# A hybrid decoder step: the recurrent heads' preparation moved beside the output gate's columns, which become two groups of four banks

## What is computed

```python
x = x + 0.5 * swiglu1(rmsnorm(x))
proj = rmsnorm(x) @ w_in          # split: q_a, k_a, v_a, f_a | qk_m, v_m, o_m, i_m, f_m
y_a = per-head rmsnorm(attention with forget gates over q_a, k_a, v_a)
qk_c = silu(causal_conv(qk_m))    # width 4, 2048 channels: 8 heads of q, 8 of k
h_m, C, n, m = mlstm(q_m, k_m, v_m, gates, state_C, state_n, state_m)
y_m = sigmoid(o_m) * per-head rmsnorm(h_m)
x = x + concat(y_a, y_m) @ w_out
x = x + 0.5 * swiglu2(rmsnorm(x))
```

## Time and profile before

| what | value |
|---|---|
| median of 3 runs | 2315.3 us (2314.76 to 2317.62) |
| the profiled execution, its time | 2320.72 us |
| its span | 2319.1 us |
| busy TensorE / VectorE / ScalarE / GpSimd | 2290.2 / 1228.4 / 842.8 / 50.3 us |
| TensorE's granted clock, mean | 0.994 |
| transfers, mean | 166 GB/s, 384.05 MB |

### The profile page before, as it was taken

How to read it: one execution, slowest core, us unless ns; L and a number is a source line. 1 busy time by engine, 2 the same in 40 slices (tenths; PEclk the granted TensorE clock), 3 DMA queues, 4 the chain that set the end, 5 groups by cost and what they waited for, 6 DMA issues and landing times.

```text
span 2319.1 us, 48002 instructions
## 1 busy us (share of the span) xinstructions
PE 2290.2 (99%) x17805; PEld 2246.8 (97%) x17805; DVE 1228.4 (53%) x1907; ACT 842.8 (36%) x1109; POOL 50.3 (2%) x84
## 2 busy tenths in 40 slices
PE   9999999999999999999999999999999999999998
PEld 8999999999999999887999989999999999999997
DVE  6554444355444455467456766755554434554443
ACT  4333333333333343334334433533333333333332
POOL 2000000000000010010000110000000000000000
PEclk9999999999999999999999999999999999999999
DMA  6555555555554444547445455455554445555443
GB/s 169 180 166 164 164 164 175 166 166 163 171 166 166 165 152 146 168 136 271 157 164 167 132 155 173 151 181 163 163 163 168 171 168 169 168 164 168 164 163 131
DMA packets 176901, 384.05 MB, mean 166 GB/s; under 512 B 19133, under 2 KB 44853, under 8 KB 176501
## 3 DMA queue, kind: packets, MB, share of 16 engines
q1 hardware_dynamic: 173888, 375.99, 50.4%
q0 software_dynamic: 2512, 5.57, 0.8%
q10 hardware_dynamic: 416, 1.32, 0.2%
HBM read 373.09 MB, written 9.70 MB: 165 GB/s over the span
## 4 chain that ended last, share of the span: by engine, by line
PE 95%; DVE 3%; ACT 1%; DMA 0%; issue 0%; SPq 0%; POOL 0%; ACTq 0%; DVEq 0%; POOLq 0%
PE ps L1788 30%; PE ps L1786 30%; PE ps L1787 29%; DVE w_lo L1010 1%; PE ps L2044 1%; DMA w_raw<-in_w_up 0%; ACT w_hi L632 0%; PE ps L2057 0%; PE ps L1856 0%; PE ps L1857 0%; PE ps L1863 0%; PE ps L1990 0%; PE ps L2337 0%; PE ps L1979 0%; PE ps L2245 0%
## 5 line engine op out<-in xcount | busy, mean ns | idle before, releaser
L1010 DVE TENSOR_TENSOR w_lo<-w_raw,w_hi 128x1024 fp32r<-128x1024 f32 (+2 forms) x698 | 789.7, 1172 | 983.9 <-ACT w_hi L632 982.5
L632 ACT CAST w_hi<-w_raw 128x1024 fp32r<-128x1024 f32 (+2 forms) x698 | 670.6, 1008 | 1290.3 <-PE ps L1788 1284.7
L1786 PE MATMUL ps<-x_hi,w_hi 128*128 128x288 f32 (+1 forms) x2752 | 813.0, 295 | 4.4 <-DVE w_lo L1010 2.6
L1788 PE MATMUL ps<-x_hi,w_lo 128*128 128x288 f32 (+1 forms) x2752 | 813.9, 296 | 0.0
L1787 PE MATMUL ps<-x_lo,w_hi 128*128 128x288 f32 (+1 forms) x2752 | 807.7, 293 | 0.0
L1786 PEld LDWEIGHTS ps<-x_hi,w_hi 128*128 128x128 f32 x2752 | 517.5, 188 | 6.3 <-DVE w_lo L1010 3.0
L1787 PEld LDWEIGHTS ps<-x_lo,w_hi 128*128 128x128 f32 x2752 | 521.2, 189 | 0.1
L1788 PEld LDWEIGHTS ps<-x_hi,w_lo 128*128 128x128 f32 x2752 | 516.5, 188 | 0.0
L1786 PE MATMUL ps<-hid_hi,w_hi 128*128 (+1 forms) x1376 | 405.6, 295 | 1.4 <-DVE X L1243 1.4
L1788 PE MATMUL ps<-hid_hi,w_lo 128*128 (+1 forms) x1376 | 407.0, 296 | 0.0
L1787 PE MATMUL ps<-hid_lo,w_hi 128*128 (+1 forms) x1376 | 403.8, 293 | 0.0
(11 more groups left out here) (487 smaller groups left out, 1438.1 us busy)
## 6 DMA issues: line engine op xcount, KB each, us to landing
w_raw<-in_w_down SPq DMA_DIRECT2D x178, 512.0 KB
w_raw<-in_w_gate SPq DMA_DIRECT2D x320, 256.0 KB
w_raw<-in_w_up SPq DMA_DIRECT2D x320, 256.0 KB
w_raw<-in_w_in SPq DMA_DIRECT2D x64, 512.0 KB
w_raw<-in_w_in SPq DMA_DIRECT2D x64, 384.0 KB
page<-in_cache_k SPq DMA_DIRECT2D x16, 512.0 KB, 4.6
w_raw<-in_w_out SPq DMA_DIRECT2D x16, 512.0 KB
w_raw<-in_w_gate SPq DMA_DIRECT2D x32, 192.0 KB
```

The lines of the kernel that those rows point to most:

```text
L632: nc.scalar.copy(w_hi[:, slot, 0:width], w_raw[:, slot, 0:width]).then_inc(w_hi_ready, 1)
L1010: nc.vector.tensor_tensor(w_lo[:, slot, 0:width], w_raw[:, slot, 0:width], w_hi[:, slot, 0:width].bitcast(F32), ALU.subtract).then_inc(w_l ...
L1786: mm(out, hi, x_hi[:, k, :], start=first and pair == 0 and s == slots[0], stop=False)
L1788: ins = mm(out, lo, x_hi[:, k, :], start=False, stop=last and pair == 1 and s == slots[-1])
```

## The change

in_m keeps three groups (q, k, v). The gate's 1024 columns become in_o, two groups of 512 columns in banks 0 to 3. The preparation is cut into pieces that stand behind banks of these groups' products and use banks 4 to 7. A step is a pair of slots, 16 in all. The convolutions, which had stood beside the groups of v and o, are now beside those of k and v: conv_tiles says which. The sigmoid of om is in two halves: the first beside step 9, the second in the third head (h = 2). qw is now made by GpSimd. Buffers on the right side of SBUF are in another order, since they lie over xm, which is still in use; state 0 is loaded as soon as w_used says that the place is free. Ws moves into counts, kws and vws into xt.

```diff
-    mixer = [("in_a", 4, KD, KD, plain[:6]), ("in_m", 4, KD, KD, plain),
+    mixer = [("in_a", 4, KD, KD, plain[:6]), ("in_m", 3, KD, KD, plain),
+             ("in_o", 2, KD, KD, plain[:4]),
...
+    def conv_tiles(t):
+        first = (0, 0, 2, 5)[t] if t < 4 else 2 * t
+        return range(first, (0, 2, 5, 8)[t] if t < 4 else first + 2)
...
         def load_out():
             load_turn(a.turn, range(SLOTS), columns(wo, 0, a.width))
+            sp.wait_ge(w_used, O_MOST)
+            load_state(0)
...
 # GpSimd
+        pool.wait_ge(w_used, O_MOST)
+        for x in qw:
+            nc.gpsimd.memset(x[:, :, :], 0.0).then_inc(sem("km_ready"), 1)
...
 # ScalarE
+            split_pair(g.turn + g.turns + (t + 1), 0, width)
+            for j in conv_tiles(t):
+                conv_silu(j)
+            split_pair(g.turn + g.turns + (t + 1), 2, width)
...
+        for step in range(16):
+            if step >= 1:
+                split_o(step + 1)
...
+            if step == 9:
+                sigmoid(0)
+            if step == 10:
+                act.wait_ge(sem("ws_logits"), 1)
+                nc.scalar.activation(Ws, Ws, ACT.Exp).then_inc(sem("ws_exp"), 1)
+            if step == 15:
+                act.wait_ge(w_used, O_MOST)
+                for i in range(2):
+                    act.wait_ge(sem("kmsT_done"), i + 1)
+                    nc.scalar.copy(kms[:, i * 512:(i + 1) * 512], ps[:, 7 - 2 * i, :]).then_inc(sem("kms_ready"), 1)
+        split_o(17)
...
             num_out(h)
+            if h == 2:
+                sigmoid(1)
 # VectorE
-        for i in range(4):
-            if i < 2:
-                split_turns(g, g.turn + i * g.turns, g.turns, UW)
+        for i in range(3):
+            width = UW if i < 2 else IN_O.width
+            if i == 0:
+                split_turns(g, g.turn, g.turns, UW)
             else:
                 for t in range(g.turns):
-                    conv((i - 2) * H + 2 * t)
-                    conv((i - 2) * H + 2 * t + 1)
+                    for j in conv_tiles((i - 1) * g.turns + t):
+                        conv(j)
...
+            if step == 7:
+                in_o_out(0)
...
+            if step == 12:
+                dve.wait_ge(w_used, O_HALF)
+                v_apart(0)
+                k_weighted(0)
+            if step == 13:
+                k_weighted(1)
+                v_apart(1)
+            if step == 14:
+                k_weighted(2)
+                k_weighted(3)
+        in_o_out(1)
+        split_o(17)
 # TensorE
+        def beside_o1(step, b):
+            if step == 0 and b == 2:
+                s_spread()
+            if step == 1 and b < 2:
+                v_natural(b, 4 + b)
+            if step == 2 and b < 2:
+                pe.wait_ge(sem("s_all_ready"), b + 1)
+                v_natural(2 + b, 6 + b)
...
+        def beside_o2(step, b):
+            if step == 2 and b == 0:
+                pe.wait_ge(sem("vws_ready"), 1)
+                pe.wait_ge(sem("ya_scaled"), 1)
+                by_sequence(vws, 0, 4, "vsT_done")
...
+        for i, beside in ((0, beside_o1), (1, beside_o2)):
+            for kt in range(IN_O.turns):
+                turn_products(IN_O, IN_O.turn + i * IN_O.turns, IN_O.index + i, kt, xm_hi, xm_lo, kt == 0,
+                              kt == IN_O.turns - 1, xr, beside)
...
         def scores(h):
...
-                pe.wait_ge(sem("kw_ready"), 2)
+                pe.wait_ge(banks_free, G_O * NBANK + 2)
```

More of the change, by code:

```diff
@@ L285, in build @@
     G_A, G_M, G_O = groups["in_a"].index, groups["in_m"].index, groups["out_a"].index
+    IN_O = groups["in_o"]
+    O_HALF, O_MOST = ((IN_O.turn + IN_O.turns + n) * 2 + 2 for n in (2, 3))
     OUT_A, OUT_B, OUT_M = groups["out_a"], groups["out_b"], groups["out_m"]
@@ L922, in _ @@
[L922 to L929 removed]
+            width = UW if t < 2 * g.turns - 1 else IN_O.width
@@ L2152, in _ @@
             turn_products(g, g.turn, g.index, kt, xm_hi, xm_lo, kt == 0, kt == g.turns - 1, xr, ya_sample_sums)
[L2153 removed]
+        with pe.Fori(1, 3) as i:
             group_products(g, i, xm_hi, xm_lo, xr)
[L2157 to L2162 removed]
@@ new lines, in v_natural, with rows_natural @@
+        def v_natural(i, bank):
+            (t, n), half = TT[i // 2], i % 2
+            for j in range(4):
+                ins = tr(ps[0:n, bank, j * P:(j + 1) * P], vm[:, 4 * half + j, t * P:t * P + n], ident[:, :])
+            ins.then_inc(sem("vT_done"), 1)
+        def rows_natural():
+            for a, row in enumerate((r_row, ws_row)):
+                for t, n in TT:
+                    ins = tr(ps[0:n, 6, (3 * a + t) * H:(3 * a + t + 1) * H], row[:, t * P:t * P + n], ident[0:H, 0:H])
+            ins.then_inc(sem("nat_done"), 1)
@@ new lines, in conv_natural, with k_natural, by_sequence @@
+        def conv_natural(i, bank):
+            for j in range(4):
+                ins = tr(ps[0:27, bank, j * P:(j + 1) * P], conv_last[:, 4 * i + j, :], ident[:, :])
+            ins.then_inc(sem("conv_rows_done"), 1)
+        def k_natural(i, bank):
+            for j in range(4):
+                ins = tr(ps[:, bank, j * P:(j + 1) * P], ext[:, H + 4 * (i % 2) + j, i // 2 * P:(i // 2 + 1) * P], ident[:, :])
+            ins.then_inc(sem("kT_done"), 1)
+        def by_sequence(src, i, bank, made):
```

313 lines of the change are left out of this document (176 added, 137 removed).

## The result

The changed kernel takes 2323.70 us by the median of 11 runs (2320.21 to 2327.35), the kernel before, timed on the same chip, 2317.56 us (11 runs, 2314.76 to 2317.98). The ratio is 1.0029 with a 95% interval of 1.0021 to 1.0037: slower by some 6 us, outside the forecast's range of 2310.8 to 2318.6. The change was timed a second time in a later session, with 2323.16 against 2316.56 and a ratio of 1.0025 (1.0016 to 1.0034). The forecast had started from 2315.3, the median of three runs; by eleven runs the same kernel's median is 2.3 us higher.

A forecast was written before the change was run, and what follows sets the result against it. TensorE, busy 2290.2 of 2319.1 us, was taken to bound the kernel. The terms -3.3 - 0.9 + 0.5 + 2.4 = -1.3 gave 2317.8, or 2314.0 as the runs' median; range 2310.8 to 2318.6.

The forecast's parts named there:

- The half clock gone, -3.3: Between input projection and head 0: vm transposes, L2168 and L2161 move between products at full clock, saving 3.3 us.
- the carry: From profile to runs: the median's 0.23% lead over the profiled execution (2315.3 against 2320.7) carries over, 2317.8 becoming 2314.0.
- Idles gone, -0.9, new idle +0.5: TensorE before head 0: two idles of 0.88 us in all go; scores(0) newly waits 0.5 us for evicted banks.
- The third convolutions, +2.4: Second in_m group, turns 2 and 3: third convolution waits for a Silu, stalling TensorE 0.9 and 1.5 us.
- rival 1: In in_m, the third convolution does not stall: -3.7 us, 2311.6; chance 0.17.
- The other pieces ... are priced the same in either place: Preparation pieces already at full clock cost the same between the gate's products; at the far end 0.9 us gain.
- I take no wait: Gate's 512-column steps: w_raw slots refill within about 4.9 us without wait; far end 5.7, using 0.8 of 0.95 slack.
- Rival 3: The gate's 512-column steps do not hold: each of 16 pays the overrun; at 0.4 us each, 2320.4; chance 0.12.
- The second sigmoid half, nothing: ScalarE in the third head: next exponential 0.8 us late, TensorE does not wait; nothing, at most 0.3.
- Rival 2: Convolution stalls in in_m also lower the clock: +0.3 us, 2315.6; chance 0.14.
- Rival 4: Moved transposes lower the clock in steps 1 to 5 to 0.50: 20 us longer, 2334; chance 0.02.

The follow-up runs named there:

- after: The changed kernel itself, against the kernel before: 2323.70 us, ratio 1.0029.
- after_again: The changed kernel timed and profiled a second time in a later session, against the kernel before: 2323.16 us, ratio 1.0025.
- stores_late: Changed kernel with GpSimd's four stores (conv_prompt, conv_sample, m_prompt, m_sample) moved to after scores(0): 2320.51 us, ratio 1.0011 to the kernel before.
- third_conv_between: Changed kernel with the third convolution behind VectorE's first subtraction, its Silu behind ScalarE's next cast: 2319.44 us, ratio 1.0006 to the kernel before.
- m_first: Changed kernel with the third convolution behind the first subtraction and both m stores issued near the start of in_m: 2318.93 us, ratio 1.0004 to the kernel before.
- before_m_early: Kernel before with its stores of m_prompt and m_sample moved ahead of the conv stores: 2320.86 us, ratio 1.0016 to the kernel before.
- two_fixed: Changed kernel with the four stores after scores(0) and the third convolution behind the first subtraction: 2321.14 us, ratio 1.0016 to the kernel before.
- before: The kernel before the change, in its first profile and timing: 2317.56 us.
- before_again: The kernel before, unchanged, profiled once more: 2315.41 us, ratio 0.9997 to the kernel before.

## Why the prediction was wrong, step by step

- **The half clock gone, -3.3: wrong in size, and this step failed first.** The forecast took the loss from one execution in which the clock had fallen for longer than it usually does: its own loss was 14.35 us, the runs of the kernel before show a mean clock of 0.9950 to 0.9956 over the sessions, which is some 10 to 12 us. And the fall moved with its products into step 0 and 1 in part of the executions. Behind the 8-row products the three profiles of the old order lost 3.4, 1.7 and 1.7 us, the ten of the new order with the same s_spread 1.7 in five and nothing in five; new falls stood behind the new waits. Over the eleven profiles with the new order 3.1 us are lost in the part of the last column on average, over the three of the old order 5.1. Over the whole program the runs' mean clocks are 0.9953 (old order) and 0.9955, 0.5 us, and by session the new order is between 0.5 us worse and 1.7 better. So the term was worth about 0.5 us in the runs and at most some 2 by the profiles, not 3.3. A mistake of the same kind lies in the carry: of the 5.4 us by which the profiled execution was above the median of three runs, some 3.4 are its surplus of falls (14.35 against 10.9), among them the very ones that were then taken away, and 2.3 come from a median of three that was low.
- **Idles gone, -0.9, new idle +0.5: right.** 0.4 was measured before scores(0).
- **The third convolutions, +2.4: right** (and rival 1, no stall, falls)**,** 2.67 by the casts and 2.64 by the experiment, each with its wait where it was put.
- **"The other pieces ... are priced the same in either place": wrong.** They cost 1.4 us more, some 0.3 for each insertion of small products; transposes of 128 rows were priced rightly at 0.45 for four.
- **"I take no wait" for the reload of w_raw: wrong.** Rival 3 had the place (a load is late) but the wrong cause and form: nothing was paid in each of 16 steps; a step with nothing beside it holds, at 3.17 us. One load is late, once, because GpSimd's stores, which the change moves, put 64 elements of 4 bytes beside it. The change part by part named SyncE's loads and TensorE's pieces and passed over GpSimd's four stores. No line of theirs changes, but they wait for conv_rows_ready, and the change raises that 40 us earlier. TensorE lost 2.2 us in after and 2.4 in after_again, where a fall of the clock stood behind it.
- **The second sigmoid half, nothing: right.** The heads keep their 4.85 us.
- **Rival 2, the convolutions' stalls cost clock: not seen.** From 1190 to 1215 the clock is 1.00 in all profiles. Behind the wait for the late load it fell in after_again and third_conv_between (1.70 us each), not in after.
- **Rival 4, the moved transposes lower the clock: wrong,** as the windows of stores_late at 1.00 show, and no profile of the new order has a fall from 1270 to 1295, where most of the transposes stand; the rule cited from the Trainium skill, "TensorE: Matmul & The Clock Gate", Part 4, did not make itself felt there.

The sum that the runs support: +2.65 (convolutions), +2.2 (late load), +1.4 (pieces), -0.5 (idles), 5.8 us in all, and some 0.5 less with the clock. The medians give 6.1 and 6.6, the stretch without the clock 216.05 less 209.75 (means of two profiles each), 6.3. Of these 6.3 some 0.5 stay open; 0.3 of it lies between the first head and the output projection.

## What to carry to other kernels

A term that removes half-clock time needs more than one profile, or the mean clock of many runs: subtract what the mean run loses. Of a moved block count every engine's queue: a store of a quarter of a kilobyte in single elements, which nobody waits for, cost more than the loads that the sum weighed. When short work is woven between long products, weave it in few, large pieces: three insertions fewer were 0.8 us less here.

## What the runs showed of the hardware

- A store of 64 elements of 4 bytes took 6.6 to 11.4 us to land, 7.1 in m_first, where no load was under way; 192 KB in rows took 2.7 to 3.3 away from the state loads and up to 6.5 beside them. Meanwhile other loads crept: 19 to 46 GB/s in before_m_early where the kernel before moved 175 to 314, a cast waited up to 5.8 us, a state load took up to 12.8.
- Falls to 1.2 GHz cost 1.70 us each or twice that (the end of the program aside), and which of the places has one changes from one execution to the next with the same program. Runs of one kernel with a mean clock of 0.995 and 0.996 differ by about 2 us, so that most of the scatter between runs is this.
- Waits of TensorE of 2.36 (two_fixed), 2.34 (after_again) and 2.84 us (third_conv_between) were followed by a fall, one of 2.06 in after by 1.00. The same wait of 2.11 us in in_a was followed by 0.68 in before and by 1.00 in before_again (995 to 1000).
- An insertion of small products between large ones costs TensorE 0.27 to 0.36 us beyond their own time; one of four 128-row transposes shows no such price (0.44 us, and 0.47 among their like).
